# Norm borders: operand made two blocks at a time, scale and bias on ScalarE, the mean taken off by GpSimd, statistics later at short stages

## The reference

```python
def rms_norm(x, w): ...                       # x / sqrt(mean(x^2) + eps) * w
h2 = rms_norm(x) * (1.0 + sc2) + sh2          # first block, before w_ff1
x  = x + g2 * (jnp.square(jax.nn.relu(h2 @ w_ff1[l])) @ w_ff2[l])
def layer_norm(x, g, b):
    mu  = jnp.mean(x, axis=-1, keepdims=True)
    var = jnp.mean(jnp.square(x - mu), axis=-1, keepdims=True)
    return (x - mu) * lax.rsqrt(var + LN_EPS) * g + b
for i in range(2):
    x = layer_norm(ALPHA * x + 0.5 * swiglu(x, gu[i, 0], down[i, 0]), ...)
    y = moba_attention(x, ...) if i == 0 else pool_mixer(x, ...)
    x = layer_norm(ALPHA * x + y, ...)
    x = layer_norm(ALPHA * x + 0.5 * swiglu(x, gu[i, 1], down[i, 1]), ...)
```

## Time and profile before

| | |
|---|---|
| median of 3 runs | 1518.98 us (1518.51 to 1521.5) |
| the profiled execution, its own time | 1525.12 us |
| its span, first to last instruction | 1522.8 us |
| granted TensorE clock, mean | 0.989 |
| busy: TensorE, weight loads | 97%, 90% |
| busy: VectorE, ScalarE, GpSimd | 73%, 55%, 12% |

### The profile page before, as it was taken

How to read it: one execution, slowest core, us unless ns; L and a number is a source line. 1 busy time by engine, 2 the same in 40 slices (tenths; PEclk the granted TensorE clock), 3 DMA queues, 4 the chain that set the end, 5 groups by cost and what they waited for, 6 DMA issues and landing times.

```text
span 1522.8 us, 25731 instructions
## 1 busy us (share of the span) xinstructions
PE 1475.5 (97%) x10189; PEld 1365.3 (90%) x10189; DVE 1114.7 (73%) x1474; ACT 839.3 (55%) x1135; POOL 184.6 (12%) x169
## 2 busy tenths in 40 slices
PE   8999998999999999999989989999999999899997
PEld 7999998889888899888989988889888898888887
DVE  7788987887877758666586697665966659886655
ACT  5655567655555446555454565554665545565543
POOL 0120003562000010000130020001300013030001
PEclk9999999999999999999999999999999999999999
DMA  8957756646445654555534335555455553445550
GB/s 328 370 212 277 262 203 228 216 150 215 191 173 202 239 219 169 191 193 193 193 132 176 137 119 213 193 194 192 146 202 196 186 186 136 152 182 195 191 194 28
DMA packets 43401, 295.94 MB, mean 194 GB/s; under 512 B 5052, under 2 KB 7228, under 8 KB 8750
## 3 DMA queue, kind: packets, MB, share of 16 engines
q1 hardware_dynamic: 40574, 280.24, 50.7%
q0 software_dynamic: 2736, 14.41, 2.7%
HBM read 291.44 MB, written 3.19 MB: 193 GB/s over the span
## 4 chain that ended last, share of the span: by engine, by line
PE 55%; DVE 7%; ACT 2%; issue 1%; DMA 0%; ACTq 0%; DVEq 0%
PE banks L708 24%; PE banks L710 12%; PE banks L723 5%; PE banks L725 4%; PE banks L726 4%; DVE w_lo L1868 2%; DVE part L1963 1%; ACT w_hi L1298 1%; DVE pw L2612 0%; DVE XS L2122 0%; PE banks L795 0%; PE banks L794 0%; PE banks L796 0%; DVE XS L1945 0%; PE banks L1205 0%
## 5 line engine op out<-in xcount | busy, mean ns | idle before, releaser
L1868 DVE TENSOR_TENSOR w_lo<-raw,w_hi 128x1024 fp32r<-128x1024 f32 x490 | 613.0, 1270 | 279.4 <-ACT w_hi L1298 275.4
L1298 ACT ACTIVATE w_hi<-raw 128x1024 fp32r<-128x1024 f32 x490 | 508.6, 1055 | 366.1 <-PE banks L710 176.9
L708 PE MATMUL banks<-H,w_hi 128*128 128x512 f32 x1504 | 522.2, 392 | 1.9 <-DVE w_lo L1868 1.9
L710 PE MATMUL banks<-H,w_lo 128*128 128x256 f32 x1504 | 420.4, 280 | 0.0
L708 PEld LDWEIGHTS banks<-H,w_hi 128*128 128x128 f32 x1504 | 282.3, 188 | 64.9 <-DVE w_lo L1868 2.8
L710 PEld LDWEIGHTS banks<-H,w_lo 128*128 128x128 f32 x1504 | 282.4, 188 | 0.0
L708 PE MATMUL banks<-HH,w_hi 128*128 128x512 f32 x480 | 166.8, 392 | 1.8 <-DVE w_lo L1868 1.8
L891 PE MATMUL banks<-H,w_lo 128*128 128x256 f32 x512 | 146.2, 286 | 2.0 <-ACT gate_a L1538 2.0
L893 PE MATMUL banks<-H,w_hi 128*128 128x256 f32 x512 | 144.1, 282 | 0.0
L894 PE MATMUL banks<-H,w_hi 128*128 128x256 f32 x512 | 144.1, 281 | 0.0
L723 PE MATMUL banks<-HH,w_lo 128*128 128x256 f32 x480 | 134.3, 280 | 0.0
(11 more groups left out here) (369 smaller groups left out, 2605.4 us busy)
## 6 DMA issues: line engine op xcount, KB each, us to landing
raw<-in_panels SPq DMA_DIRECT2D x265, 1024.0 KB, 4.8
rows<-cum_rows POOLq DMA_DIRECT2D x16, 384.0 KB, 4.6
late_w<-in_panels POOLq DMA_DIRECT2D x4, 1024.0 KB, 5.1
bias_rows<-rev POOLq DMA_DIRECT2D x1, 2048.0 KB, 11.4
XS<-in_x_t SPq DMA_DIRECT2D x4, 256.0 KB, 5.3
near<-bias_rows POOLq DMA_DIRECT2D x8, 128.0 KB, 3.4
out_t<-XS SPq DMA_DIRECT2D x4, 256.0 KB, 2.6
ws<-in_ws_t POOLq DMA_DIRECT2D x1, 512.0 KB, 11.3
```

The source lines that it names most:

```text
L708: pe.matmul(bank, w_hi[:, panel_slot, at:at + P], operand[:, kk, :, :].rearrange("p a t -> p (a t)"), start=starts and c == chunks[0], sto ...
L710: return pe.matmul(bank[:, 0:T], w_lo[:, panel_slot, at:at + P], operand[:, kk, 0, :], start=False, stop=stops and c == chunks[-1])
L1298: act.activation(w_hi[:, sl, w], raw[:, r, w], ACT.Copy).then_inc(panel_hi, 1)
L1868: vec.tensor_tensor(w_lo[:, sl, w], raw[:, r, w], w_hi[:, sl, w], ALU.subtract).then_inc(panel_lo, 1)
```

## The change

- `first_group` on VectorE: `scaled` and `lo` handle two blocks in one instruction; the norm's scale is no longer in them, and the mean is no longer taken off by VectorE. `scaled` is x times root, `lo` is the full value less the rounded one.
- ScalarE: per block two instructions in place of one, with scale and bias in both: H's rounded part and, in place, the full value. The halves of panels 2 and 3 stand ahead of blocks 0, 2, 4, 6. At centred borders ScalarE then makes four blocks of shift, edge 0 times (mean times root) plus edge 1, into the other half of `ev`, ahead of the table load and of panel 4.
- VectorE's group 0: PSUM times root into `first` (which frees PSUM), then plus the shift. Silu and what follows need no edges any more.
- GpSimd: `mean_off`, 4 additions of 128x512 with the negative mean, once the last `unscaled_lo` is done; no bias additions at these borders. It now adds blocks 1 to 3 into `part` at out, att_out and pool_out as well.
- TensorE: `whole_stats` comes after block 3 at out and pool_out, after block 4 (the first of the second panel) at att_out, elsewhere after block 1 as before.
- Modulation panels stand behind every second panel of ff2.
- `att_scores` waits for another semaphore, which now tells that group 0 is complete.

```diff
+STATS_BEHIND = {"out": 3, "ff2": 1, "down0": 1, "att_out": 4, "down1": 1, "pool_out": 3}
+SUMMED_BY_POOL = {name: BANKS + (name in SUMMED_AHEAD) for name in NORMED}
@@ gpsimd
+            def mean_off(i):
+                name = CENTRED[i]
+                pool.wait_ge(S["mean_kept"], [n for n in UNSCALED_ORDER if n in CENTRED].index(name) + 1)
+                pool.wait_ge(S["unscaled_lo"], unscaled_count(name, KD - 1))
+                away = st[:, 0, :].unsqueeze(1).to_broadcast([P, 2, T])
+                for a in range(KD // 2):
+                    two = slice(2 * a, 2 * a + 2)
+                    pool.tensor_tensor(xb[:, two, :], xb[:, two, :], away, ALU.add).then_inc(S["norm_centred"], 2)
...
-            add_first_group(3)
-            for i in range(6):
-                if NORMED[i + 2] in SUMMED_AHEAD:
-                    add_first_group(4 + i)
...
+            add_first_group("ff2")
+            for i, name in enumerate(CENTRED):
+                add_first_group(name)
...
+                elif name in AHEAD_OF_NORM:
+                    mean_off(i)
@@ tensor, unscaled_group
-                        last.then_inc(half_used, 1)
-                        if p == 0 and half == 0:
-                            whole_stats(stage)
+                                if b == BANKS - 1 and c % 2:
+                                    last.then_inc(half_used, 1)
+                            if k == STATS_BEHIND[stage]:
+                                whole_stats(stage)
@@ scalar, first_group
                     for m in range(KD):
-                        if m in (1, 2, 4, 6):
-                            at = (1, 2, 4, 6).index(m)
-                            split(q + at // 2, *raw_place(q + at // 2), halves=(at % 2,))
+                        if m % 2 == 0:
+                            split(q + m // 4, *raw_place(q + m // 4), halves=(m // 2 % 2,))
                         act.wait_ge(S["norm_y"], KD * k + m + 1)
...
-                            ins = act.activation(H[:, m, 0, :], src[:, m, :], ACT.Identity, bias=bias[:, m:m + 1])
+                            hi = act.activation(H[:, m, 0, :], src[:, m, :], ACT.Identity, bias=bias[:, m:m + 1],
+                                                scale=scale[:, m:m + 1])
+                            full = act.activation(src[:, m, :], src[:, m, :], ACT.Identity, bias=bias[:, m:m + 1],
+                                                  scale=scale[:, m:m + 1])
...
+                    if stage_name in CENTRED:
+                        act.wait_ge(S["edges_kept"], edges_count(stage_name))
+                        for b in range(BANKS):
+                            act.activation(ev[:, 1 - G, b, :], st[:, 3, :], ACT.Identity, bias=edges[:, b, 1:2],
+                                           scale=edges[:, b, 0:1]).then_inc(S["shift_ready"], 1)
                     rest(s, G, lambda half: split(q + SPLIT, *raw_place(q + SPLIT), halves=(half,)))
@@ vector, last_group_unscaled
-                adds = {3: (5, 6)} if alone else {0: (1, 2), 1: (3,), 2: (4, 5), 3: (6,)} if name == "att_out" else \
-                    {1: (4,), 2: (5,), 3: (6,)}
+                adds = {1: (4,), 2: (5,), 3: (6,)} if name in ("out", "pool_out") else {3: (4, 5, 6)}
@@ vector, first_group
+                def scaled(a):
+                    if mean:
+                        vec.wait_ge(S["norm_centred"], KD * (k - 3) + 2 * a + 2)
+                    two = slice(2 * a, 2 * a + 2)
+                    vec.tensor_tensor(dest[:, two, :], xb[:, two, :], st[:, 2, :].unsqueeze(1).to_broadcast([P, 2, T]), ALU.mult)\
+                        .then_inc(S["norm_y"], 2)
...
+                    vec.tensor_tensor(H[:, two, 1, :], dest[:, two, :], H[:, two, 0, :], ALU.subtract).then_inc(S["norm_lo"], 2)
...
-                        for g in range(2):
-                            vec.tensor_tensor(by_group(xb)[:, g, :, :], by_group(xb)[:, g, :, :], away, ALU.add)\
-                                .then_inc(S["norm_centred"], BANKS)
...
+                    for a in range(KD // 2 + 1):
+                        if a < KD // 2:
+                            scaled(a)
+                        if a:
+                            lo(a - 1)
+                        if a < KD // 2:
+                            split_half(q + a // 2, a % 2)
+                    if mean:
+                        vec.tensor_tensor(st[:, 3, :], st[:, 0, :], st[:, 2, :], ALU.mult)
...
+                    vec.tensor_tensor(first, group_banks(G), root, ALU.mult).then_inc(taken, 1)
                     if mean:
-                        vec.wait_ge(S["edges_kept"], [n for n in UNSCALED_ORDER if n != "ff2"].index(stage_name) + 1)
-                        for b in range(BANKS):
-                            last = vec.scalar_tensor_tensor(first[:, b, :], st[:, 0, :], edges[:, b, 0:1],
-                                                            banks[:, BANKS * G + b, 0:T], ALU.mult, ALU.add)
-                        last.then_inc(taken, 1)
+                        vec.wait_ge(S["shift_ready"], BANKS * ([n for n in UNSCALED_ORDER if n in CENTRED].index(stage_name) + 1))
                         vec.wait_ge(taken, FIRST_GROUP[s] + 1)
-                        vec.tensor_tensor(first, first, root, ALU.mult).then_inc(S["first_scaled"], 1)
+                        vec.tensor_tensor(first, first, ev[:, 1 - G, :, :], ALU.add).then_inc(S["first_scaled"], 1)
@@ vector, split_and_mods
-                if 0 <= late < LATE:
-                    mod_panel(MODS_IN_GATES + late)
+                if 0 <= late < 2 * LATE and late % 2 == 0:
+                    mod_panel(MODS_IN_GATES + late // 2)
```

More of the change, by code:

```diff
@@ L101, with parts_before @@
 EDGE = 2
+STATS_BEHIND = {"out": 3, "ff2": 1, "down0": 1, "att_out": 4, "down1": 1, "pool_out": 3}
+SUMMED_BY_POOL = {name: BANKS + (name in SUMMED_AHEAD) for name in NORMED}
+def parts_before(name):
+    return sum(SUMMED_BY_POOL[n] - 1 for n in NORMED[:NORMED.index(name)])
 WIDE = ("ff1", "gu0", "gu1", "gu2", "gu3")
@@ L347, in unscaled_count, with edges_count @@
             return KD * UNSCALED_ORDER.index(name) + m + 1
+        def edges_count(name):
+            return [n for n in UNSCALED_ORDER if n != "ff2"].index(name) + 1
         def norm_scale(name):
@@ L668, in add_first_group @@
                 total = part[:, :, :]
-                for b in range(1, 5):
+                for b in range(1, SUMMED_BY_POOL[name]):
                     if b > 1:
@@ L1432, in post, with first_relu2 @@
                     rest(s, G, lambda half: split(q + SPLIT, *raw_place(q + SPLIT), halves=(half,)))
                 return post
[L1435 to L1445 removed]
+            def first_relu2(s, G, next_half):
+                act.wait_ge(S["first_scaled"], UNSCALED_ORDER.index(BEFORE_STAGE[STAGES[s][0]]) + 1)
+                for b in range(BANKS):
+                    act.activation(ev[:, G, b, :], ev[:, G, b, :], ACT.Identity, bias=edges[:, b, 0:1]).then_inc(S["first_kept"], 1)
+                next_half(0)
+                next_half(1)
+                round_into(HH)(s, 0, G)
@@ L1999, in last_group @@
                     return
-                alone = name in SUMMED_AHEAD
-                adds = {3: (5,)} if alone else {1: (1, 2), 2: (3,), 3: (4,), 4: (5,)} if name == "att_out" else {2: (4,), 3: (5,)}
                 for b in range(BANKS + 1):
-                    if b == BANKS - 1 and alone:
-                        vec.wait_ge(S["norm_part"], BANKS * SUMMED_AHEAD.index(name) + BANKS)
-                    for m in adds.get(b, ()):
-                        add_block(name, m)
-                    if b == BANKS - 1 and name != "att_out":
+                    if b == BANKS - 1:
+                        vec.wait_ge(S["norm_part"], parts_before(name) + SUMMED_BY_POOL[name] - 1)
+                        add_block(name, KD - 3)
                         add_square(name)
@@ L2042, in take_up @@
                     last.then_inc(taken, 1)
-                    if name not in SUMMED_AHEAD:
-                        for m in (1, 2, 3):
-                            add_block(name, m)
                 def split_and_low(q, *place, halves=(0, 1)):
@@ L2192, in first_glu @@
                 vec.wait_ge(activated, before("activated", s) + 1)
[L2193 to L2202 removed]
+                vec.scalar_tensor_tensor(ev[:, G, 0:2, :], ev[:, G, 0:2, :], 0.5, ev[:, G, 2:BANKS, :], ALU.mult, ALU.mult)\
+                    .then_inc(multiplied, 1)
                 next_half(1)
[L2204 to L2206 removed]
+                lo_into(HH[:, 0:22, :, :], 2)(s, 0, G)
             def first_keep(s, G, next_half):
```

139 lines of the change are left out of this document (42 added, 97 removed).

## The result

The changed kernel took 1536.08 us (median of 4 runs) against 1520.24 of the kernel before on the same chip: ratio 1.009 (95% interval 1.0061 to 1.0119). Run again, unaltered, it took 1533.93 against 1518.94 (1.0091, 1.0075 to 1.0107). By the ratios it is slower by 14 us, between the medians by 15 to 16; the forecast of 1518 and the range up to 1526 were wrong.

The account below looks back on a forecast made before the run. TensorE, busy 97%, was taken as the bound, with a chain from t0 to panel 4 at centred borders. 4.6-1.2-1.6+3.3-4+0+0=+1.1 us gained gave 1518, called no change; range 1504 to 1526.

Parts of the forecast that it names:

- t0: At each border, the start of the variance (L2139), from which the prediction counted the chain to panel 4's rest.
- per two blocks one half panel 0.95 and four of 0.40: ScalarE's order at centred borders, setting the pace if GpSimd's additions cost VectorE nothing: last `lo` at t0+12.9.
- 3.0 to 4.0 us off the chain: At out, VectorE's shorter body and no waits for ScalarE shorten the chain to panel 4's rest; +3.3 after collision.
- Waits under 2 us left no lower clock: TensorE's clock: only waits of 3 us and more cost another 1.5 to 3 us.
- gu2's -1.2: At gu2, panel 4's rest done at 1097.6 against 1096.4, a loss of 1.2 us; with bound 0, +2.3.
- att_out, -4: At gu1, GpSimd's additions and statistics waiting for block 4 delay panel 4's rest: -4 us, bounds -7.3 and +2.
- the bound of strict alternation: At att_out, VectorE and GpSimd strictly taking turns: last addition ends at 888.0, against 884.35 without collision; 886.2 taken.
- the second rival: At att_out, GpSimd's three additions collide fully with `U_early`'s rests: gu1 -7.3, total 1521 to 1525; chance 0.20.
- Mean on GpSimd, 5.2 us of VectorE's time: At centred borders, GpSimd's four `mean_off` additions exclude VectorE: 5.2 us, bounds 0 and 5.2.
- the exchange in ff2: In ff2, the DMA wait goes (+2.0), but the last panel's later rest brings 2.0 of waiting: 0, bounds -1 and +2.
- the longer tail with the table load: At gu1 to gu3, a table load (1.28) between shifts and panel 4 makes panel 4's rest 1.2 us later.
- The first rival: GpSimd's additions cost VectorE little: half the cost gives +11 (1508), none +18 (1501); chance 0.30.

Follow-up runs that it names:

- Bias left out: The changed kernel with the mean taken off by VectorE, and ScalarE's two instructions per block keeping the scale without the bias: 1520.86 us (0.9994).
- Mean on GpSimd with the faster ScalarE: The changed kernel with only the norm's scale given back to VectorE's product, block by block; the mean stays on GpSimd: 1525.52 us (1.0040).

## Why the prediction was wrong

It had the right frame (TensorE's work and a chain from t0 to panel 4) and the right places, and sized that chain too short. By place, gain predicted and gain measured between the two profiles: qk +4.6, +3.3; gu2 -1.2, -3.8; gu3 -1.6, -2.6; out +3.3, 0.0; gu1 -4, -6.6; ff2 0, -1.4; gu0 0, 0. In sum +1.1 against -11.1; the spans differ by 9.4, since the changed kernel's profile reached the first border 1.7 us sooner.

- **The failed step: "per two blocks one half panel 0.95 and four of 0.40".** The 0.40 was taken from instructions with a bias alone and carried over to instructions with bias and scale. They take 0.49 in a row, two blocks 2.92 and not 2.55, four pairs 1.5 us more; the four shifts 2.1 and not 1.7. The last `lo` waits for ScalarE and ends at t0+17.25 for 16.5, and panel 4's rest ends at t0+23.5, not 22.4. I had looked for the price of this engine only where it was a bound. With the mean on VectorE the price is worth 13 us ("Bias left out"), with the mean on GpSimd, as in the change, 8 ("Mean on GpSimd with the faster ScalarE"). The Trainium skill, ScalarE: Activation LUTs, in its section on what ACT_TABLE_LOAD costs, gives 186 ns and 0.833 ns per element, and about 93 ns more for each operand that is a pointer to one number per partition; an estimate by that rule is 492 ns for 128x256 with one pointer and 586 with two, and the trace agrees (495 and 590).
- **"3.0 to 4.0 us off the chain" at out** was 1.1, for the same reason: with the scale back on VectorE it ends another 1.7 us sooner. And the step forgot that TensorE comes earlier by what it no longer waits: it wanted panel 4 at 25.2 us after group 0's start and not at 29.1, and found it 1.9 late. A wait that is taken away moves the need for everything behind it.
- **No term for the clock.** "Waits under 2 us left no lower clock" was true of the one profile. Behind the waits of 1.8 and 1.9 us the clock fell to half in one profile (0.83 over 10 us) and stayed full in the other, at the same two places. And gu2's -1.2 made a wait of 1.7 into one of 2.9 and put nothing behind it, though the prediction itself had 1.5 to 3 us behind waits of 3 us and more. TensorE then stood 0.8 us for H and 3.06 for panel 4, with half clock behind it: of the 2.6 us by which gu2 missed, 1.1 are the later panel 4, and the other 1.5 are put down to the clock by subtraction.
- **att_out, -4** was right in sign and mechanism. The end of the last addition was to be at +8.1 from group 0's start, with +9.9 as the bound of strict alternation; it was at 9.4. From there to t0 I had 4.0 us; with TensorE's slow start behind its 4.6 of standstill it was 5.3. That is nearer to the second rival, "the collision at att_out in full", than to the forecast: the last addition ended past its limit (887, which is +8.9), TensorE stood 4.6 us for its 4.8, the clock was at half from 884.1 to 887.4, and gu1 lost 6.6 for its 7.3. It doesn't explain the total: all of it undone gives 4 of the 14 us back. The Trainium skill, SBUF - State Buffer, on the two separate sides, was the basis of the bound; the trace agrees with it here too, in three pairs out of three.
- **Mean on GpSimd, 5.2 us of VectorE's time** was 4.2, less the 2.3 of its own, which makes 1.9; the first `lo` came 1.35 later, and 1.8 with the faster ScalarE. Right, and the time showed none of it until ScalarE was faster.
- **Right**: the exchange in ff2 (one wait of 1.8 for another), the longer tail with the table load, the statistics later than 890 at att_out in the forecast's frame, waits for panel 4 at gu1 to gu3 (1.65, 3.06, 1.49). Not foreseen: such a wait at qk too (1.65), and 2.1 us each for H at gu1 and gu3. The first rival (GpSimd costs little) is refuted.

The parts don't add up as single numbers: ScalarE's price undone gives 13 us or 8, panel 4's order 13, and putting back the statistics of out and pool_out costs nothing or 3.6 to 4.6 us, by what stands behind them. That "Bias left out" comes out at the forecast's time (0.9994) is partly luck: with the mean where the change has it, the kernel with the faster ScalarE is still at 1.0040.

## What to carry to other kernels

Before work is moved to an engine with idle time, price the instruction in the exact form that it will have there (kind and number of operands), and count the order behind it: a chain is paced by its slowest engine per step, not by the busiest over the span. When a wait is taken out, work out anew when the waiting engine will want each later thing. Put what the bound engine needs first ahead of what merely comes first in the data flow: moving one half panel past four small instructions was worth about 5 us in the kernel before.

## What the runs showed of the hardware that I had not expected

- ScalarE: 128x256 with a number per channel for scale and one for bias takes 590 ns, with either alone 495.
- VectorE and GpSimd with two SBUF inputs each took turns in every pair shown, one instruction each, so that short ones of VectorE lost most: 0.40 became 1.45, 1.22 became 2.31. A `TENSOR_SCALAR` of VectorE with a single input (128x256, 0.29 in the kernel before) took 1.20 beside GpSimd's additions.
- A standstill of TensorE of 1.9 us was followed by full clock in one execution and by half clock for a third of 10 us (0.83) in another of the same kernel, at the same place.
- A chain shorter by 1.7 us at the borders gave 14.5 us in all, up to half of it through the granted clock (0.9895 to 0.994).
